# A mixture-of-experts decoder step on one core: gate/up weights in 16 KB runs, tokens gathered three expert blocks at a time

## The chip, the core and the metric

One core of a Trainium2 chip runs the whole step as one program. The metric is the device time of one execution in microseconds; the time of a kernel is the median of its runs. TensorE (PE) multiplies, VectorE (DVE), ScalarE (ACT) and GpSimd (POOL) work on tiles in SBUF and on TensorE's results in PSUM, SyncE (SP) only issues DMAs. Sixteen DMA engines move data between HBM and SBUF; each moves one contiguous piece, a packet in the profile, at a time.

## The reference, cut to what matters

One layer of a hybrid decoder over 336 rows (16 meta tokens and 256 prompt tokens, 8 sequences of 8 new tokens). A state-space branch and an attention branch are merged, projected and added to the residual; then a routed mixture of experts follows:

```python
hn = rmsnorm(h, norm2_g)                       # 336 x 1024
gsel = argmax(hn @ w_rg + b_rg)                # 1 of 4 groups
topl, topi = top_k(el_sel, 2)                  # 2 of its 8 experts
def block(tok, wr, e):                         # the rows that chose expert e
    xb = hn[tok]
    hb = silu(xb @ w_gate[e]) * (xb @ w_up[e])     # 1024 -> 512, twice
    return (hb @ w_down[e]) * wr[:, None]          # 512 -> 1024
```

There are 32 experts; everything is float32. An expert has 2.097 MB each of gate, up and down weights, 6.29 MB in all, and each expert in use is read once.

## The kernel before, in words

The program runs phases one after another: setup, state-space branch, attention, merge (`merge_phase`), routing (`route_phase`), experts (`moe_phase`) and the final norm. The 336 rows lie in three tiles of 128, 128 and 80 rows.

**Ahead of the experts.** `merge_phase` ends with the second norm. VectorE scales each row tile into `hn` (line 1318, named yT in the profile, whose memory it uses), waiting for GpSimd's root per tile (line 1279); TensorE transposes `hn` (1367), VectorE multiplies by `norm2_g` (1323) and TensorE computes the router's logits (1374). `norm2_g` comes to SBUF as 8 rows of 128 numbers in one of ten small loads on ScalarE's queue (line 188), for all of which TensorE waits at the very start; a transpose turns them into columns of `gcol`. `route_phase` chooses the experts and gives each pair of token and expert a slot: blocks of 64 slots, each block owned by one expert; GpSimd's iota instructions (1411 to 1418) are waited for there. In the input at hand 32 blocks are in use, one per expert.

**Weights.** SyncE issues all weight loads on one queue. `load_gate_up` (line 1534) issues two DMAs per expert, gate and up; partition p gets the rows p, 128 + p, 256 + p, ... of the 1024 x 512 matrix, that is eight pieces of 2 KB. `load_down` (1541) gives partition p rows of 1024 numbers, four pieces of 4 KB. There are three buffers for gate/up (the third lies in a reused tile named stretch) and two for down. The first three gate/up pairs and two downs are loaded ahead, by guess of the expert's number. Then `load(b, h)` (1601) issues block b's down once block b-2's results have been copied out (`y_ev`, line 1605), and block b+2's gate/up once block b-1's products have been read (`gu_free`, 1609); the first of these is block 3's (1614).

**A block.** All of it is unrolled per engine, with semaphores between the engines. TensorE: 8 x 2 products of gate/up into `ph` (1721); `gather_rows` for the next block, 3 x 2 products with a 0/1 matrix `block_rows` that picks the block's 64 rows of `hn` (1699, into px); two transposes of the hidden rows (1728); `gather_turn`, four transposes of the picked rows (1706); then 4 x 2 products with `w_down` (1736), after waiting for h_t, for the weights and for a free result bank. A float32 product shows as two records. Two products of 64 result rows each run side by side in the two halves of the array. ScalarE: tanh (1638), the copy of the picked rows px out of PSUM (1630), the copy of the result (1642) and its store, two DMAs of 128 KB. VectorE: `pick()` builds the next 0/1 matrix by comparing slots with an iota (1659, 1664); h_gate and h_rows (1681, 1684); the copy of h_t (1687); the scaling of the gathered, transposed rows by `norm2_g` (1669). Before the loop `pick`, `gather_rows(1)` and `gather_turn(1)` run once by themselves.

Of the kernel before, what the change touches and what calls it, by code (L numbers as in the profile page):

```python
# [14 lines left out]
F32 = mybir.dt.float32  # L15
# [6 lines left out]
P = 128  # L22
# [36 lines left out]
LEAST_BLK = 2 * T // BLK // 2 * 2  # L59


def bc(ap, shape):

    return ap.to_broadcast(list(shape))


def setup_phase(nc, A, S, sem):

    with ExitStack() as ctx:
# [3 lines left out]
        rows64 = tsb("param_rows", [64, P])  # L73
# [110 lines left out]
        def _(act):  # L184
# [3 lines left out]
            act.dma_start(rows64[56:64, :], A["norm2_g"].rearrange("a (t p) -> (a t) p", p=P)).then_inc(par_in, 16)  # L188
# [28 lines left out]
        def _(v):  # L217
# [9 lines left out]
            v.tensor_copy(S["gcol"][:, :], ps[6][:, 32:64])  # L227
# [70 lines left out]
        def _(pe):  # L298
            pe.wait_ge(consts, 1)
            pe.wait_ge(par_in, 160)  # L300
            pe.transpose(ps[6][:, 0:64], rows64[:, :], S["ident"][0:64, 0:64])
# [916 lines left out]
def merge_phase(nc, A, S, sem):  # L1218

    with ExitStack() as ctx:  # L1220
# [27 lines left out]
        def _(sp):  # L1248
# [12 lines left out]
            sp.dma_start(wr[:, :, 0:4], A["w_router_group"].rearrange("a (t p) c -> p (a t) c", p=P)).then_inc(wr_in, 16)  # L1261
            sp.dma_start(wr[:, :, 4:36], A["w_router_expert"].rearrange("a (t p) c -> p (a t) c", p=P)).then_inc(wr_in, 16)
# [33 lines left out]
        def _(v):  # L1296
# [19 lines left out]
            for t, r in enumerate(ROWS):  # L1316
                v.wait_ge(rs_ok, 3 + t + 1)
                v.tensor_scalar(S["hn"][0:r, t, :], S["xtok"][0:r, t, :], ss[0:r, t:t + 1], None,
                                ALU.mult).then_inc(hn_ok, 1)
            for t, r in enumerate(ROWS):  # L1320
                for h in range(2):
# [3 lines left out]
                                    bc(S["gcol"][:, 24 + 4 * h:28 + 4 * h].unsqueeze(2), [P, 4, r]),  # L1325
# [53 lines left out]
def route_phase(nc, A, S, sem):  # L1379


    with ExitStack() as ctx:
# [4 lines left out]
        it64i, itbi, itb = tsb("iota64_i", [P, BLK], I32), tsb("iota_blk_i", [1, NBLK], I32), tsb("iota_blk", [1, NBLK])  # L1387
# [158 lines left out]
def moe_phase(nc, A, S, sem):  # L1546
# [4 lines left out]
    with ExitStack() as ctx:  # L1551
        def tsb(name, shape, dt=F32):
# [4 lines left out]
        eq = tsb("slot_eq", [P, 3, 2, BLK])  # L1557
        sel = tsb("block_rows", [P, 3, BLK])
        xrow = tsb("x_rows", [P, 512])
        xg = tsb("x_gathered", [P, 4, 2, BLK])  # L1560
# [3 lines left out]
        px, pxt, ph, pht = (ctx.enter_context(nc.psum_tensor(n, [P, 512], F32)) for n in ("px", "pxt", "ph", "pht"))  # L1564
        py = [ctx.enter_context(nc.psum_tensor(f"py{h}", [P, 512], F32)) for h in range(2)]
        sel_ok, xr_ps, xr_ev, xt_ps, xt_ok, gu_ps, th_ok, hb_ok, ht_ps, ht_ok, y_ps, y_ev, gu_free = (
            sem(n) for n in ("sel_ok", "xrow_ps", "xrow_ev", "xt_ps", "xt_ok", "gu_ps", "hth_ok", "h_ok", "ht_t_ps",
# [5 lines left out]
        block = ctx.enter_context(nc.Block())  # L1573

        def blocks_of(eng):
            return eng.value_load(S["blk_e"][0:1, NBLK:NBLK + 1], min_val=1, max_val=NBLK)

# [46 lines left out]
        def _(act):  # L1624
            nblk = blocks_of(act)
            act.sem_inc(y_ev, 2)

            def rows_out(n):
                act.wait_ge(xr_ps, n)
                act.activation(xrow[:, :], px[:, :], ACT.Copy).then_inc(xr_ev, 1)  # L1630

            rows_out(1)
# [19 lines left out]
        def _(v):  # L1652
# [3 lines left out]
            def pick():  # L1656
# [3 lines left out]
                                bc(S["iota"][:, :].unsqueeze(1), [P, 6, BLK]),  # L1660
                                bc(rel[:, :, :].rearrange("p t j -> p (t j)").unsqueeze(2), [P, 6, BLK]),
# [3 lines left out]
                v.tensor_scalar(rel[:, :, :], rel[:, :, :], -float(BLK), None, ALU.add)  # L1665

            def gathered(n):
                v.wait_ge(xt_ps, n)
                v.tensor_tensor(xg[:, :, :, :], pxt[:, :].rearrange("p (c j s) -> p c j s", c=4, j=2),  # L1669
                                bc(S["gcol"][:, 24:32].rearrange("p (j c) -> p c j", j=2).unsqueeze(3),  # L1670
                                   [P, 4, 2, BLK]), ALU.mult).then_inc(xt_ok, 1)

            pick()
            gathered(1)
            with v.Fori(0, NBLK // 2) as i:
                for u in range(2):
                    b = 2 * i + u
                    with v.If(b < nblk):
                        pick()
# [5 lines left out]
                                               ALU.mult).then_inc(hb_ok, 1)  # L1685
                        v.wait_ge(ht_ps, b + 1)
                        v.tensor_copy(ht[:, :, :, :], pht[:, 0:256].rearrange("p (c j s) -> p c j s", c=2, j=2)
                                      ).then_inc(ht_ok, 1)
                        gathered(b + 2)

        @block.tensor
        def _(pe):
            nblk = blocks_of(pe)

            def gather_rows(n):
                pe.wait_ge(sel_ok, n)
                for t, r in enumerate(ROWS):
                    for j in range(2):
                        mm = pe.matmul(px[64 * j:64 * j + 64, :], sel[0:r, t, :], S["hn"][0:r, t, 512 * j:512 * j + 512],  # L1699
                                       start=(t == 0), stop=(t == 2))  # L1700
                mm.then_inc(xr_ps, 1)

            def gather_turn(n):
                pe.wait_ge(xr_ev, n)
                for c in range(4):
                    mm = pe.transpose(pxt[:, P * c:P * c + P], xrow[:, P * c:P * c + P], S["ident"][:, :])
                mm.then_inc(xt_ps, 1)
# [193 lines left out]
```

## Time and profile before

| what | before |
|---|---|
| median of 3 runs, us | 1550.07 (1548.98 to 1555.38) |
| span of the profiled execution, us | 1547.8 |
| PE busy / DVE / ACT / POOL | 87% / 32% / 17% / 13% |
| granted clock of TensorE, mean | 0.925 of full |
| SyncE's DMA queue | 232242 packets, 302.03 MB, 57.6% of 16 engines |
| issues of 2 MB expert weights | 32 gate, 32 up, 32 down |

The span reaches from the first to the last instruction of the profiled execution, and is the only time given for that execution; the median of the runs is 2.3 us longer. In the rows below, a line such as L1721 is a line of the kernel, `out<-in` names the tiles, "128*64 128x512" is a weight load of 64 columns with 512 moving columns, and a count stands behind x. SPq and ACTq are DMA issues on the queues of SyncE and ScalarE; their duration is the time the issue took, not the transfer. A granted clock of 1.00 is 2.4 GHz, 0.50 is 1.2 GHz.

### The profile page before, as it was taken

Reading aid. Unit: us, or ns where it says so; the run is one execution under the profiler, and the core shown is the slowest. Engines: PE = TensorE matmul, PEld = TensorE weight load, DVE = VectorE, ACT = ScalarE, POOL = GpSimd, SP = SyncE. Lnnn points to the kernel's source line nnn. Section 1 sums busy time; section 2 is a strip of 40 time slices with the busy share of each in tenths; the row PEclk is TensorE's granted clock in tenths of the full one; section 3 lists DMA queues with packets and bytes.
Section 4 is the critical chain, followed back from the end, with each engine's and each line's share of the span. In section 5 each row is a group of like instructions: output and inputs, shape, how many; then the busy total and the mean of one; then the engine's idle time right before and its main releaser. Section 6 shows DMA issues by size and latency. Waiting matters only on the chain. (4 is left out here: it accounts for less than half of the span.)

```text
span 1547.8 us, 19560 instructions
## 1 busy us (share of the span) xinstructions
PE 1339.0 (87%) x6097; PEld 738.9 (48%) x6097; DVE 492.3 (32%) x1106; ACT 263.9 (17%) x677; POOL 205.9 (13%) x401
## 2 busy tenths in 40 slices
PE   5799999999995997786999998499998899998990
PEld 3676667666672555554666654233332233332330
DVE  2245555556545673332000002421212112111113
ACT  1132223322330442221000000011100000010011
POOL 3032443334432120000000000000000000000003
PEclk9799999999996998998999999599999999999995
DMA  6033234424222238454865700789999999999974
GB/s 191 19 109 112 85 94 126 139 78 118 81 58 70 50 99 299 136 157 101 221 136 126 219 21 0 272 335 396 395 398 395 395 398 395 395 398 395 395 291 125
DMA packets 241057, 318.30 MB, mean 206 GB/s; under 512 B 21010, under 2 KB 148434, under 8 KB 241026
## 3 DMA queue, kind: packets, MB, share of 16 engines
q1 hardware_dynamic: 232242, 302.03, 57.6%
q10 hardware_dynamic: 6736, 8.94, 1.7%
q0 software_dynamic: 2048, 6.95, 1.7%
q8 instruction: 16, 0.26, 0.1%
q14 instruction: 15, 0.12, 0.0%
HBM read 289.20 MB, written 28.68 MB: 205 GB/s over the span
## 5 line engine op out<-in xcount | busy, mean ns | idle before, releaser
L667 PE MATMUL psg<-stretch 128*128 128x336 f32 x512 | 159.8, 477 | 11.3 <-DVE h_sample_out L645 9.6
L1736 PE MATMUL py<-w_down,h_t 128*64 128x512 f32 x512 | 135.6, 679 | 30.4 <-DMA w_down<-in_w_exp_down 30.4
L1721 PE MATMUL ph<-w_gate_up,x_gathered 128*64 128x512 f32 x704 | 157.2, 600 | 0.9 <-DVE x_gathered L1669 0.9
L667 PEld LDWEIGHTS psg<-stretch 128*128 128x128 f32 x512 | 103.7, 204 | 69.2 <-DVE h_sample_out L645 15.4
L1681 DVE SCALAR_TENSOR_TENSOR h_gate<-h_tanh,ph 128x256 f32<-128x256 f32 x32 | 13.5, 421 | 339.1 <-ACT h_tanh L1638 339.1
L1699 PE MATMUL px<-yT,block_rows 128*64 128x512 f32 (+1 forms) x396 | 93.3, 607 | 10.7 <-DVE block_rows L1664 10.7
L1721 PEld LDWEIGHTS ph<-w_gate_up,x_gathered 128*64 128x64 f32 x704 | 50.8, 139 | 104.1 <-issue 104.1
L582 DVE SCALAR_TENSOR_TENSOR x_conv<-x_padded,conv_wh,x_conv 128x360 f32<-128x360 f32 x96 | 57.0, 594 | 100.9 <-ACT x_conv L531 90.0
L1736 PEld LDWEIGHTS py<-w_down,h_t 128*64 128x64 f32 x512 | 38.3, 154 | 105.5 <-issue 69.9
L676 PE MATMUL psg<-stretch 128*128 128x256 f32 (+1 forms) x384 | 84.5, 380 | 0.0
L1343 PE MATMUL psm<-stretch,w_merge 128*128 128x336 f32 x256 | 76.2, 457 | 6.9 <-DMA w_merge<-in_w_in 6.9
L1773 POOL DMA_INDIRECT y_expert<-expert_rows,slot_i x6 | 5.7, 958 | 549.2 <-PEq L1743 547.7
L676 PEld LDWEIGHTS psg<-stretch 128*128 128x128 f32 (+1 forms) x384 | 67.3, 177 | 14.5
L1348 PE MATMUL psm<-yT,w_merge 128*128 128x336 f32 x256 | 73.6, 446 | 0.0
L1721 PE MATMUL ph<-stretch,x_gathered 128*64 128x512 f32 x320 | 70.4, 592 | 0.0
L1343 PEld LDWEIGHTS psm<-stretch,w_merge 128*128 128x128 f32 x256 | 49.9, 196 | 31.6 <-issue 8.9
L1304 DVE SCALAR_TENSOR_TENSOR mix_part<-gate_tanh,psm 128x336 f32<-128x336 f32 x16 | 7.3, 501 | 178.5 <-PE psm L1351 178.5
L1699 PEld LDWEIGHTS px<-yT,block_rows 128*64 128x64 f32 (+1 forms) x396 | 28.8, 140 | 68.2 <-issue 57.4
L1348 PEld LDWEIGHTS psm<-yT,w_merge 128*128 128x128 f32 x256 | 48.6, 190 | 23.7
L1091 PE MATMUL psa<-stretch,w_q 128*128 128x336 f32 x128 | 42.0, 486 | 15.0 <-DVE k_and_c L1000 12.6
L1642 ACT ACTIVATE y_block<-py 128x512 f32<-128x512 f32 x32 | 19.1, 597 | 192.2 <-PE py L1736 192.2
L1638 ACT ACTIVATE h_tanh<-ph 128x256 f32<-128x256 f32 x32 | 12.3, 384 | 203.4 <-PE ph L1721 203.4
(414 smaller groups left out, 1777.8 us busy)
## 6 DMA issues: line engine op xcount, KB each, us to landing
w_down<-in_w_exp_down SPq DMA_DIRECT2D x32, 2048.0 KB, 19.1
w_gate_up<-in_w_exp_gate SPq DMA_DIRECT2D x22, 2048.0 KB, 19.1
w_gate_up<-in_w_exp_up SPq DMA_DIRECT2D x22, 2048.0 KB, 22.9
stretch<-in_w_exp_gate SPq DMA_DIRECT2D x10, 2048.0 KB, 19.2
stretch<-in_w_exp_up SPq DMA_DIRECT2D x10, 2048.0 KB, 23.2
stretch<-in_w_in SPq DMA_DIRECT2D x16, 1024.0 KB, 5.3
stretch<-in_w_in SPq DMA_DIRECT2D x16, 512.0 KB, 7.5
h<-in_state_ssm SPq DMA_DIRECT2D x16, 512.0 KB, 4.9
```

What stands on the lines that cost most here:

```text
L582: i = v.scalar_tensor_tensor(xc[:, m, :], xp[:, m, w:w + 360], S["conv_wh"][:, w, bass.ds(o, 1)], xc[:, m, :], ALU.mult, ALU.add)
L667: mm = pe.matmul(ps[m][:, 0:T], wg[:, k, P * m:P * m + P], S["xnT"][:, k, :], start=(k == 0), stop=(k == KT - 1))
L676: mm = pe.matmul(ps[4 + t // 2][0:r, 256 * (t % 2):256 * (t % 2) + 256], S["xnT"][:, k, COL[t]:COL[t] + r], wg[:, k, 512:768], start=(k == ...
L1091: mm = pe.matmul(ps[0][:, 0:T], wq[:, k, :, :], S["xnT"][:, k, :], start=(k == 0), stop=(k == KT - 1))
L1343: mm = pe.matmul(ps[4 * h + j][:, 0:T], wm[h][:, 8 * j + k, :], S["xnT"][:, k, :], start=(k == 0), stop=(k == KT - 1))
L1348: pe.matmul(ps[4 * h + 2][:, 0:T], wm[h][:, 16 + k, :], S["yT"][:, k, :], start=(k == 0), stop=(k == 15))
L1638: act.activation(th[:, :], ph[:, 0:256], ACT.Tanh, scale=0.5).then_inc(th_ok, 1)
L1642: act.activation(yr[h][:, :], py[h][:, :], ACT.Copy).then_inc(y_ev, 1)
L1681: v.scalar_tensor_tensor(hg[:, :], th[:, :], 1.0, ph[:, 0:256], ALU.add, ALU.mult).then_inc(gu_free, 1)
L1699: mm = pe.matmul(px[64 * j:64 * j + 64, :], sel[0:r, t, :], S["hn"][0:r, t, 512 * j:512 * j + 512], start=(t == 0), stop=(t == 2))
L1721: mm = pe.matmul(ph[64 * j:64 * j + 64, :], xg[:, k % 4, k // 4, :], w_gu[w][:, :, k, 256 * j:256 * j + 256], start=(k == 0), stop=(k == K ...
L1736: mm = pe.matmul(py[h][64 * j:64 * j + 64, :], ht[:, k % 2, k // 2, :], w_dn[h][:, k, 512 * j:512 * j + 512], start=(k == 0), stop=(k == 3))
```

## The change

The rows of gate and up are dealt out differently: partition p now gets rows 8p to 8p+7, which lie behind one another in memory, so a load has one run of 16 KB per partition. The column order of `hn` follows (column k of partition p is 8p + k), by a strided read when `hn` is scaled, and so do the router's weights and `norm2_g`, which is now loaded directly as columns (`gcol2`). `load_down` is as before.

The gather is made for chunks of three blocks (192 slots) at once and without the turn: `hn` is the stationary operand, the 0/1 matrix of 192 columns the moving one, and the result arrives transposed, eight slices k of 128 partitions x 192 columns, three products each. The slices are dealt into six groups, two per block: one between gate/up and the transposes of the hidden rows, one between these and `w_down`. Two PSUM banks px0 and px1 alternate; VectorE scales each group into one of two buffers `x_gathered`. ScalarE's copy px to x_rows and TensorE's four transposes go. `pick` runs once per three blocks with three times the columns. Before the loop the whole first chunk is gathered.

```diff
+CHUNK = 3
+COLS = CHUNK * BLK
+GROUPS = ((0, 2), (2, 1), (3, 2), (5, 1), (6, 1), (7, 1))
...
-            act.dma_start(rows64[56:64, :], A["norm2_g"].rearrange("a (t p) -> (a t) p", p=P)).then_inc(par_in, 16)
+            act.dma_start(S["gcol2"][:, :], A["norm2_g"].rearrange("a (p t) -> (a p) t", p=P)).then_inc(par_in, 16)
...
-            sp.dma_start(wr[:, :, 4:36], A["w_router_expert"].rearrange("a (t p) c -> p (a t) c", p=P)).then_inc(wr_in, 16)
+            sp.dma_start(wr[:, :, 4:36], A["w_router_expert"].rearrange("a (p t) c -> p (a t) c", p=P)).then_inc(wr_in, 16)
...
-                v.tensor_scalar(S["hn"][0:r, t, :], S["xtok"][0:r, t, :], ss[0:r, t:t + 1], None,
+                v.tensor_scalar(S["hn"][0:r, t, :].rearrange("r (k p) -> r k p", k=KT),
+                                S["xtok"][0:r, t, :].rearrange("r (p k) -> r k p", k=KT), ss[0:r, t:t + 1], None,
                                 ALU.mult).then_inc(hn_ok, 1)
...
-            pool.iota(it64i[:, :], pattern=[[1, BLK]], base=0, channel_multiplier=0)
+            pool.iota(it64i[:, :], pattern=[[1, COLS]], base=0, channel_multiplier=0)
...
-        eng.dma_start(S["w_gate_up"][h][:, j, :, :], A[w].rearrange("a e (t p) f -> p (a e) t f", p=P)[
-            :, bass.ds(e, 1)].rearrange("p o t f -> p (o t) f")).then_inc(done, 16)
+        eng.dma_start(S["w_gate_up"][h][:, j, :, :].rearrange("p t f -> p (t f)"), A[w].rearrange("a e (p t) f -> p (a e) (t f)", p=P)[
+            :, bass.ds(e, 1)].rearrange("p o f -> p (o f)")).then_inc(done, 16)
...
+        def bank(g):
+            k0, n = GROUPS[g]
+            return px[g % 2][:, 0:n * COLS].rearrange("p (k s) -> p k s", k=n)
...
-                        rows_out(b + 2)
...
+            def gathered(chunk, parity, g):
+                k0, n = GROUPS[g]
+                v.wait_ge(xg_ps, n_groups * chunk + g + 1)
+                v.tensor_tensor(xg[parity][:, k0:k0 + n, :], bank(g),
+                                bc(S["gcol2"][:, k0:k0 + n].unsqueeze(2), [P, n, COLS]), ALU.mult).then_inc(xg_ok, 1)
 
             pick()
-            gathered(1)
-            with v.Fori(0, NBLK // 2) as i:
-                for u in range(2):
-                    b = 2 * i + u
+            for g in range(n_groups):
+                gathered(0, 0, g)
+            pick()
+            with v.Fori(0, NBLK // 6) as i:
+                for u in range(6):
+                    b, chunk, a, parity = 6 * i + u, 2 * i + u // 3 + 1, 2 * (u % 3), (u // 3 + 1) % 2
                     with v.If(b < nblk):
-                        pick()
                         v.wait_ge(th_ok, b + 1)
...
+                        gathered(chunk, parity, a)
                         v.wait_ge(ht_ps, b + 1)
...
-                        gathered(b + 2)
+                        gathered(chunk, parity, a + 1)
+                        if u % 3 == 2:
+                            pick()
...
+            def gather(chunk, g):
+                k0, n = GROUPS[g]
+                if g == 0:
+                    pe.wait_ge(sel_ok, chunk + 1)
+                pe.wait_ge(xg_ok, n_groups * chunk + g - 1)
+                for k in range(n):
+                    for t, r in enumerate(ROWS):
+                        mm = pe.matmul(bank(g)[:, k, :], S["hn"][0:r, t, P * (k0 + k):P * (k0 + k) + P],
+                                       sel[0:r, t, :], start=(t == 0), stop=(t == 2))
+                mm.then_inc(xg_ps, 1)
...
-                                mm = pe.matmul(ph[64 * j:64 * j + 64, :], xg[:, k % 4, k // 4, :],
+                                mm = pe.matmul(ph[64 * j:64 * j + 64, :],
+                                               xg[u // 3][:, k, BLK * (u % 3):BLK * (u % 3) + BLK],
                                                w_gu[w][:, :, k, 256 * j:256 * j + 256],
                                                start=(k == 0), stop=(k == KT - 1))
                         mm.then_inc(gu_ps, 1)
-                        gather_rows(b + 2)
+                        gather(chunk, a)
                         pe.wait_ge(hb_ok, b + 1)
...
-                        gather_turn(b + 2)
+                        gather(chunk, a + 1)
                         pe.wait_ge(ht_ok, b + 1)
```

## Rows read from the trace of the kernel before

**Rows 1.** The page, the span in 40 equal slices: GB/s moved.

```profile
GB/s 191 19 109 112 85 94 126 139 78 118 81 58 70 50 99 299 136 157 101 221 136 126 219 21 0 272 335 396 395 398 395 395 398 395 395 398 395 395 291 125
```

**Rows 2.** Busy time by stretch (us busy, instructions), granted clock, DMA share, GB/s.

```profile
960.00:1000.00 40.00, 19.72 (x84) 14.62 (x86) 15.18 (x59) 1.01 (x3) 1.40 (x7) 0.50 0.71 263
1000.00:1010.00 10.00, 10.00 (x38) 3.08 (x36) 0.99 (x4) 0.38 (x1) 0.00 (x0) 0.79 0.00 0
...
1060.00:1460.00 400.00, 364.89 (x1628) 122.67 (x1624) 71.85 (x170) 38.80 (x75) 0.00 (x0) 0.95 1.04 396
...
985.00:988.00 3.00, 0.00 (x0) 0.00 (x0) 2.85 (x4) 0.00 (x0) 0.00 (x0) 0.50 1.02 405
...
989.50:993.50 4.00, 2.14 (x6) 0.77 (x8) 1.26 (x4) 0.00 (x0) 0.00 (x0) 0.50 1.04 386
```

**Rows 3.** Waits of 1000 to 1547 us: us in total, times, longest one.

```profile
PE py L1736 <- DMA w_down<-in_w_exp_down: 30.4, 22, 2.1
```

**Rows 4.** Timeline of a block: start us, us, engine, line, tiles, [idle before].

```profile
1016.24 7.04 PE L1721 MATMUL ph<-w_gate_up,x_gathered 128*64 128x512 f32 x32
...
1023.10 2.75 PE L1699 MATMUL px<-yT,block_rows 128*64 128x512 f32 x12
...
1024.25 0.42 DVE L1684 SCALAR_TENSOR_TENSOR h_rows<-h_gate,ph 128x256 f32<-128x256 f32 x1
...
1025.78 0.44 PE L1728 MATMUL pht<-ident,h_rows 128*128 128x128 f32 x2
...
1027.14 3.65 PE L1736 MATMUL py<-w_down,h_t 128*64 128x512 f32 x16
...
1030.62 0.60 PE L1721 MATMUL ph<-stretch,x_gathered 128*64 128x512 f32 x2
```

**Rows 5.** Timeline of SyncE's queue: five gate/up issues and one w_down.

```profile
970.79 3.98 SPq L1542 DMA_DIRECT2D w_down<-in_w_exp_down  x1
974.81 2.10 SPq L1537 DMA_DIRECT2D stretch<-in_w_exp_gate  x1
...
1009.96 0.39 SPq L1537 DMA_DIRECT2D w_gate_up<-in_w_exp_gate  x1
...
1100.99 1.62 SPq L1537 DMA_DIRECT2D w_gate_up<-in_w_exp_gate  x1
...
1464.45 1.63 SPq L1537 DMA_DIRECT2D w_gate_up<-in_w_exp_gate  x1
1466.19 7.93 SPq L1537 DMA_DIRECT2D w_gate_up<-in_w_exp_up  x1
```

**Rows 6.** DMA issues, 965 to 1000 us: KB each, us to landing.

```profile
w_down<-in_w_exp_down SPq DMA_DIRECT2D x1, 2048.0 KB, 18.2
stretch<-in_w_exp_gate SPq DMA_DIRECT2D x1, 2048.0 KB, 19.6
```

**Rows 7.** TensorE groups by line and shape: busy us, mean ns, idle.

```profile
L676 PE MATMUL psg<-stretch 128*128 128x256 f32 x256 | 56.8, 380 | 0.0
...
L1351 PE MATMUL psm<-stretch,w_merge 128*128 128x336 f32 x128 | 37.5, 446 | 0.0
```

**Rows 8.** Timeline of 990 to 1000 us: first selection, first row products, first block.

```profile
990.31 0.56 DVE L1659 TENSOR_TENSOR slot_eq<-iota,slot_rel 128x384 f32<-128x384 f32 x1
990.94 0.36 DVE L1664 TENSOR_TENSOR block_rows<-slot_eq 128x192 f32<-128x192 f32 x1
...
991.36 5.39 PE L1699 MATMUL px<-yT,block_rows 128*64 128x512 f32 x12 [10.66 <-DVE block_rows L1664]
...
999.42 9.47 PE L1721 MATMUL ph<-w_gate_up,x_gathered 128*64 128x512 f32 x32 [0.86 <-DVE x_gathered L1669]
```

**Rows 9.** Timeline: scaling of the third row tile; a small first load.

```profile
955.90 0.75 DVE L1318 TENSOR_SCALAR yT<-xtok,ss 80x1024 f32<-80x1024 f32 x1 [0.86 <-POOL ss L1279]
...
5.39 0.80 ACTq L193 DMA_DIRECT2D brow<-in_b_forget  x1
```

**Rows 10.** The page, DMA queues: packets, MB, share of 16 engines over the span.

```profile
q8 instruction: 16, 0.26, 0.1%
```

More of the change, by code:

```diff
@@ L71, in tsb @@
             return ctx.enter_context(nc.sbuf_tensor(name, shape, dt))
-        rows64 = tsb("param_rows", [64, P])
+        rows64 = tsb("param_rows", [56, P])
         convw_rows = tsb("convw_rows", [P, P])
@@ L1556, in moe_phase @@
         rel = tsb("slot_rel", [P, 3, 2])
[L1557 to L1560, printed above, removed]
+        eq = tsb("slot_eq", [P, 3, 2, COLS])
+        sel = tsb("chunk_rows", [P, 3, COLS])
+        xg = [tsb(f"x_gathered{c}", [P, KT, COLS]) for c in range(2)]
         th, hg, hrow = tsb("h_tanh", [P, 256]), tsb("h_gate", [P, 256]), tsb("h_rows", [P, 256])
@@ L1563, in moe_phase @@
         yr = [tsb(f"y_block{h}", [P, 512]) for h in range(2)]
-        px, pxt, ph, pht = (ctx.enter_context(nc.psum_tensor(n, [P, 512], F32)) for n in ("px", "pxt", "ph", "pht"))
+        ph, pht = (ctx.enter_context(nc.psum_tensor(n, [P, 512], F32)) for n in ("ph", "pht"))
+        px = [ctx.enter_context(nc.psum_tensor(f"px{h}", [P, 512], F32)) for h in range(2)]
         py = [ctx.enter_context(nc.psum_tensor(f"py{h}", [P, 512], F32)) for h in range(2)]
-        sel_ok, xr_ps, xr_ev, xt_ps, xt_ok, gu_ps, th_ok, hb_ok, ht_ps, ht_ok, y_ps, y_ev, gu_free = (
-            sem(n) for n in ("sel_ok", "xrow_ps", "xrow_ev", "xt_ps", "xt_ok", "gu_ps", "hth_ok", "h_ok", "ht_t_ps",
+        sel_ok, xg_ps, xg_ok, gu_ps, th_ok, hb_ok, ht_ps, ht_ok, y_ps, y_ev, gu_free = (
+            sem(n) for n in ("sel_ok", "xg_ps", "xg_ok", "gu_ps", "hth_ok", "h_ok", "ht_t_ps",
                              "ht_ok", "yb_ps", "yb_ev", "gate_up_free"))
@@ L1659, in pick @@
                 v.tensor_tensor(eq[:, :, :, :].rearrange("p t j c -> p (t j) c"),
-                                bc(S["iota"][:, :].unsqueeze(1), [P, 6, BLK]),
-                                bc(rel[:, :, :].rearrange("p t j -> p (t j)").unsqueeze(2), [P, 6, BLK]),
+                                bc(S["iota"][:, :].unsqueeze(1), [P, 6, COLS]),
+                                bc(rel[:, :, :].rearrange("p t j -> p (t j)").unsqueeze(2), [P, 6, COLS]),
                                 ALU.is_equal)
@@ L1693, in _ @@
             nblk = blocks_of(pe)
[L1695 to L1707, printed above, removed]
-            gather_rows(1)
-            gather_turn(1)
+            def gather(chunk, g):
[8 more added lines that the diff above has]
+                mm.then_inc(xg_ps, 1)
+            pe.wait_ge(sel_ok, 1)
+            for g, (k0, n) in enumerate(GROUPS):
+                if g > 1:
+                    pe.wait_ge(xg_ok, g - 1)
+                for k in range(n):
+                    for t, r in enumerate(ROWS):
+                        mm = pe.matmul(bank(g)[:, k, :], S["hn"][0:r, t, P * (k0 + k):P * (k0 + k) + P],
+                                       sel[0:r, t, :], start=(t == 0), stop=(t == 2))
+                mm.then_inc(xg_ps, 1)
             with pe.Fori(0, NBLK // 6) as i:
@@ L1713, in _ @@
                     b, h, w = 6 * i + u, u % 2, u % 3
+                    chunk, a = 2 * i + u // 3 + 1, 2 * (u % 3)
                     with pe.If(b < nblk):
-                        pe.wait_ge(xt_ok, b + 1)
+                        if u % 3 == 0:
+                            pe.wait_ge(xg_ok, n_groups * chunk)
                         pe.wait_ge(w_ok, b + 1)
@@ L1815, in sb @@
             S[name] = stack.enter_context(nc.sbuf_tensor(name, shape, dt))
-        for name, shape in (("ident", [P, P]), ("ones", [P, P]), ("mhalf", [P, 4]), ("gcol", [P, 32]),
+        for name, shape in (("ident", [P, P]), ("ones", [P, P]), ("mhalf", [P, 4]), ("gcol", [P, 24]), ("gcol2", [P, KT]),
                             ("xtok", [P, 3, D]), ("yT", [P, 16, T]), ("topw", [P, 3, 2]), ("slot", [P, 3, 2]),
-                            ("iota", [P, BLK])):
+                            ("iota", [P, COLS])):
             sb(name, shape)
```

22 lines of the change are left out of this document (7 added, 15 removed).

## The prediction, made before the changed kernel was run

> **What bounds the kernel now.** I read the page's forty slices first, for which resource is flat. From the 28th slice the bytes per second stand at 395 to 398 for eleven slices in a row [rows 1]; nothing ahead of them is so even. Second, busy time by stretch: from 1060 to 1460 us the DMA engines are busy throughout (a share of 1.04, since packets overlap) and move 396 GB/s, while TensorE is busy for 365 of 400 us at a granted clock of 0.95; from 1000 to 1010 nothing is moved at all [rows 2]. Third, the waits: TensorE waits 22 times, 30.4 us, for `w_down` [rows 3]. Fourth, one block before the DMA falls behind: gate/up to gate/up takes 1030.62 - 1016.24 = 14.38 us at full clock [rows 4]. Fifth, SyncE's issues: from the 7th gate load (1100.99) to the 29th (1464.45) lie 22 blocks in 363.46 us, 16.52 us each, and one up load holds the queue for 7.93 us, which I read as a queue that is full [rows 5]. So a block needs 14.38 us of TensorE and gets its weights every 16.52 us. The expert stage, a third of the span, is bound by the rate at which weights arrive. It runs at that pace from the first load after the prefetch, at 1009.96 [rows 5], which is when block 0's gate/up products have been read. From there 29 gate and 29 up loads follow one another without a hole; the tail behind them the change leaves as it is.
>
> **Gate/up runs of 16 KB.** Each 2.097 MB load keeps its bytes and goes from 1024 pieces of 2 KB to 128 of 16 KB: from 64 pieces to 8 on each of 16 engines. What a piece costs must come from pieces of different length. The prefetch before the stage gives it, with no other traffic and TensorE all but idle. By issue plus landing time, `w_down` (4 KB runs, 32 pieces per engine) lands at 970.79 + 18.2 = 989.0, the third slot's gate (2 KB) at 974.81 + 19.6 = 994.4, so the stretch 985 to 988 is `w_down` alone and 989.5 to 993.5 the gate alone: 405 against 386 GB/s [rows 2, 5, 6]. A load therefore takes 5.178 us at 4 KB and 5.433 us at 2 KB; 0.255 us for 32 pieces is 8.0 ns a piece. At 8 pieces a load would take 5.178 - 24 x 0.0080 = 4.99 us (420 GB/s, an extrapolation by four in length). Saving: 0.446 us a load, x 58 = **-25.9 us**. Bounds: if nothing is gained beyond 4 KB, 0.255 x 58 = -14.8; if each of the two rates is off by 1 GB/s so that they lie further apart, the same working gives some -28.5. The check: two gate/up loads, one `w_down` and 0.26 MB of result rows at the 2 KB rate make 16.72 us against the 16.52 observed. After the change the block's transfers need 16.52 - 0.89 = 15.63 us.
>
> The row puts the step from 2 to 4 KB at 4.9%. The Trainium skill ("DMA: Bandwidth & Descriptors", Why small descriptors are slow) says that a packet costs about 3 extra cycles beside one per 32 bytes. That is 67 cycles for 64 at 2 KB and 515 for 512 at 16 KB; by it a load falls from 5.433 to an estimated 5.22 us, 58 of them save 12.4 us, and the step to 4 KB should have been 2.3%: the trace shows twice that.
>
> **Gathering three blocks at once.** It lies on TensorE, VectorE and ScalarE, under the transfers. Removed per block: six row products (from 1023.10 to the h transposes at 1025.78, 2.68 us), four transposes behind them (of the 1.36 us to 1027.14, 0.6), ScalarE's copy. Added per three blocks: 24 products of 192 columns. The nearest rows are 256 columns, 56.8 us for 128 products (two records each), 0.444 us, and 336 columns, 37.5 for 64, 0.586 us [rows 7]; the line through them gives 0.33 us at 192. The first two blocks of three get nine, 14.38 - 2.68 - 0.6 + 2.97 = 14.07 us; the third gets six, of which only three (0.99 us) cover the chain tanh, h_gate, h_rows that ends at 1024.67, 1.57 us after gate/up [rows 4], so TensorE stands 0.6 to 0.7 us: 13.74. Mean 13.96 us, under the 15.63 of the transfers: **0**. Low clock must be added: a clock of 0.95 over 400 us is 40 us at half speed, 20 us lost over 24 blocks, 0.8 each; 14.8 is still below 15.63. If that cover went (low clock twice as often), TensorE would set the pace near 15.6, where the forecast is anyway. VectorE's new wait for the gathered columns stands ahead of its copy of h_t, for which TensorE waits: in a nine-product block the columns are there some 2.0 us after gate/up, scaling 384 costs about 0.56 like the 384 of [rows 8], the copy 0.42 like h_rows; that ends near 3.0, when TensorE (2.0 + 0.44 + 0.99) is still in its second group. In the third block the group is half as long. VectorE is busy 72 of 400 us [rows 2] and has room. On SyncE the order of loads and waits stays; shorter lists of pieces fill its queue less, and it then waits for `gu_free` or `y_ev` instead, with only the next load behind it.
>
> **The first gather.** This one nothing hides: no load is in flight from 1000 to 1010, and every microsecond delays 1009.96. The two selection instructions have three times the elements: 384 cost 0.56 and 192 cost 0.36 us, so 1152 and 576 cost 1.36 and 0.76, +1.2 us [rows 8]. Then 24 products where 12 records in 5.39 us, a copy, transposes and a scaling took until 999.42 [rows 8]. The clock was 0.50 up to 1000, and 0.79 from 1000 to 1010 [rows 2], so it rose near 1004.2, 4.8 us after gate/up began. If it rises 4.8 us into the new unbroken stream: 7.3 products at 0.66 and 16.7 at 0.33 take 10.3 us; block 0 begins at 991.36 + 1.2 + 10.3 + 0.6 (last scaling) = 1003.5 and ends, at full speed, 7.04 later, 1010.5, against 999.42 + 9.47 = 1008.9 now: +1.6. If it stays low: 15.8 us for the gather, 9.47 for block 0, +9.5. I take **+3**, near the first because the pauses between 996.75 and 999.42, in which the old stream waited for the copy and the scaling, are gone.
>
> **Serial edits.** The scaling of the rows reads every eighth column. 1024 contiguous columns take 0.75 us and the third instruction waits 0.86 us for GpSimd [rows 9]; at one element a cycle, which VectorE's 1.04 ns per element [rows 8] shows, 1024 would take 1.1 to 1.3: the first two eat the slack, the third adds 0.5. **+0.8**, between 0 and, if the stride halves the rate again, +3.5. The norm2_g load becomes 128 pieces of 32 B among ten small loads that TensorE waits for; a broadcast load of as many pieces takes 0.80 us to issue [rows 9], and less was spent before: +0.3, ends 0 and +0.8. GpSimd's wider iota and cast stand before the routing: all its work in those 40 us is 1.40 us [rows 2], so at most a few tenths, +0.2. The router's weights are loaded long before their use: 0. **Tail:** TensorE's last block is some 0.4 us shorter: -0.4.
>
> **Sum.** -25.9 + 3 + 1.3 - 0.4 = -22.0 us. The profiled execution's span is 1547.8 us, so its new span is 1525.8. The median of the runs is 1550.07, 2.3 us above that span; I keep this and forecast **1528 us**.
>
> **Rivals.** *Runs stop paying at 4 KB* (the engines cut a longer run, or something else caps near 405): -14.8 + 3.9 = -10.9, 1539. For it: no load of this kernel shows more than 405 in an undisturbed stretch. Chance 0.14. *The overhead is half of what I read*, because 3 us of `w_down` are a small sample: 12.9 saved, 1541; 0.07. By the 3-cycle rule of the Trainium skill ("DMA: Bandwidth & Descriptors", Why small descriptors are slow) this one would be the forecast. *The bytes set the rate, not the pieces*: then no load gets shorter and the start and serial edits remain, +3.9, 1554. Against it stand 405 and 386 in one trace; 0.07. The Trainium skill ("DMA: Bandwidth & Descriptors", Where 436 GB/s comes from) says that HBM, at about 358 GB/s a core, binds such loads; by it 1554 would be right, but the 396 GB/s held here for 400 us lie above its limit. *Slower: a 16 KB piece is served worse.* The place is each gate/up load. The only 16 KB packets in the trace are the instruction queue's: 16, 0.26 MB, 0.1% of 16 engines' span [rows 10]; 0.1% is 24.8 us, 1.55 us a packet, and with the rounding at least 0.77 us, 339 GB/s over 16 engines. A load would take 6.19 us, 58 x 0.76 = +44, 1598 at the least. Against it: those packets shared their engines with other queues and go elsewhere. It decides from 5.46 us a load (384 GB/s): above that, 58 x 0.03 + 3.9 pass 0.5%. Chance 0.08. *More than forecast*: a piece costs more than 8 ns, or the clock rises at once, 1518; 0.05. That leaves 0.59 for the forecast.
>
> **Numbers.** A measurement of this kernel can tell 0.5%, 7.75 us, from no change: below 1542.3 is faster, above 1557.8 slower. Faster: 0.59 + 0.14 x 0.9 + 0.07 x 0.6 + 0.05 = 0.80. Slower 0.08. Same 0.12: the no-gain case and the edges of the two small ones. Range 1517 to 1542: the forecast with its bounds (-28.5 + 1.6 up to -14.8 + 3.9), the 4 KB case, about half of the 1541 case and most of the 1518 case hold some 0.8.
>
> **What would show it.** Right: steady slices near 16.52/15.63 x 396 = 419 GB/s, 57,344 fewer packets, gate loads 15.6 us apart, TensorE still waiting for `w_down`, about 1.6 us a block less the low clock, block 0's gate/up starting at 1003 to 1006. The 4 KB rival would show 408; no gain, 396; the slow one, less, with longer waits. Wrong: waits at `w_down` gone and blocks 15 us or more apart (TensorE bound), the first load past 1016, or a gap in the loads.

## The result, and the profile after

The changed kernel takes 1526.01 us, the median of four runs (1524.47 to 1528.54), beside 1550.44 (1548.98 to 1555.38) for the kernel before: a ratio of 0.984, 95% interval 0.982 to 0.986. The forecast was 1528, the range 1517 to 1542. The span of the profiled execution went from 1547.8 to 1522.8 us, 25.0 less.

First the forty slices of the changed kernel's page, GB/s moved, beside [rows 1].

```profile
GB/s 194 19 111 101 99 83 141 114 86 97 127 59 58 49 47 306 150 155 66 257 134 138 116 187 0 151 234 422 424 420 427 419 426 421 426 421 423 425 301 127
```

The plateau is still there and still flat, so the same resource bounds the stage; it stands at 419 to 427 where it stood at 395 to 398. The windows say the same beside [rows 2] (per engine us busy and instructions, then granted clock, DMA share, GB/s):

```profile
1000.00:1010.00 10.00, 9.38 (x51) 7.71 (x52) 4.75 (x9) 0.00 (x0) 0.00 (x0) 0.95 0.09 35
1010.00:1060.00 50.00, 49.73 (x246) 24.69 (x244) 10.36 (x23) 3.33 (x7) 0.00 (x0) 1.00 0.87 354
1060.00:1460.00 400.00, 364.21 (x1728) 165.40 (x1726) 72.34 (x157) 25.52 (x52) 0.00 (x0) 0.98 1.02 423
```

423 GB/s in the steady stretch against 396; TensorE busy for 364 us as before, but for more blocks. SyncE's queue moved the same 302.03 MB in 174,898 packets instead of 232,242: 57,344 fewer, 896 for each of the 64 loads. Next the waits from 1000 to 1547 us (us in total, times, longest), beside [rows 3]:

```profile
DVE x_gathered L1672 <- PE px L1708: 29.9, 54, 0.8
...
PE py L1749 <- DMA w_down<-in_w_exp_down: 33.3, 19, 2.1
...
PE pht L1741 <- DVE h_rows L1687: 2.8, 10, 0.3
```

TensorE still waits for `w_down`, no less than before: both sides of the race became faster. The one large new wait is VectorE's for the gathered columns, and nobody is late for it: h_t and the hidden rows are waited for 2.8 us in all. One block, beside [rows 4], in the timeline of TensorE, of the changed kernel:

```profile
1021.70 7.07 PE L1733 MATMUL ph<-w_gate_up,x_gathered 128*64 128x512 f32 x32
1028.70 2.22 PE L1708 MATMUL px<-chunk_rows,yT 128*128 128x192 f32 x12
1030.76 0.38 PE L1741 MATMUL pht<-ident,h_rows 128*128 128x128 f32 x2
1030.98 1.14 PE L1708 MATMUL px<-chunk_rows,yT 128*128 128x192 f32 x6
1032.09 3.65 PE L1749 MATMUL py<-w_down,h_t 128*64 128x512 f32 x16
1035.55 7.07 PE L1733 MATMUL ph<-stretch,x_gathered 128*64 128x512 f32 x32
1042.54 1.24 PE L1708 MATMUL px<-chunk_rows,yT 128*128 128x192 f32 x6
1044.06 0.44 PE L1741 MATMUL pht<-ident,h_rows 128*128 128x128 f32 x2 [0.27 <-DVE h_rows L1687]
```

Gate/up to gate/up takes 13.85 us where it took 14.38. The third block of a chunk (from 1035.55) has the short first group, and there TensorE stands 0.27 us for the hidden rows. SyncE's queue, beside [rows 5]: the 1st, 7th and 29th gate load, one up load, and the load that ends the stage (`final_g`, the final norm's vector, issued when SyncE is through with the expert stage).

```profile
1015.98 0.35 SPq L1541 DMA_DIRECT2D w_gate_up<-in_w_exp_gate  x1
...
1097.98 0.33 SPq L1541 DMA_DIRECT2D w_gate_up<-in_w_exp_gate  x1
...
1435.69 0.33 SPq L1541 DMA_DIRECT2D w_gate_up<-in_w_exp_gate  x1
1436.12 0.38 SPq L1541 DMA_DIRECT2D w_gate_up<-in_w_exp_up  x1
...
1493.65 0.36 SPq L1771 DMA_DIRECT2D final_g<-in_final_norm_g  x1
```

The first loads are 13.67 us apart (six intervals in 82.00 us), TensorE's pace, while the prefetched stock lasts; the 7th to the 29th lie 15.35 us apart, the 13th to the 29th 15.50 (16.52 before). No up load holds the queue any longer: 0.38 us to issue, not 7.93. Reading note: the median from issue to landing rose from 19 to 23 or 24 us for a gate load, though the stage moves more bytes per second. I read that as an earlier start of the count: an issue no longer waits for room in the queue, so it is made while earlier loads are still under way.

The accounting of the 25.0 us uses two marks, the first gate load (1009.96 before [rows 5], 1015.98 now) and the issue of `final_g`. Of the kernel before it needs three more lines, the start of the scaling, the copy of the slots and `final_g`:

```profile
953.64 1.41 DVE L1318 TENSOR_SCALAR yT<-xtok,ss 128x1024 f32<-128x1024 f32 x2
...
990.06 0.17 DVE L1654 COPY slot_rel<-slot 128x6 f32<-128x6 f32 x1 [1.22 <-PEq L1382]
...
1518.41 0.36 SPq L1758 DMA_DIRECT2D final_g<-in_final_norm_g  x1
```

From the first gate load to the issue of `final_g`, which I call the stage, it was 1518.41 - 1009.96 = 508.45 us and is 477.67: **-30.8**. The first load itself went from 1009.96 to 1015.98: **+6.0**. Behind `final_g`: -0.2. Of the +6.0, 3.45 are there before any edited instruction of this part runs: the scaling of `hn` starts at 957.09 instead of 953.64, and in the other profiles below it starts anywhere from 952.42 to 961.58, with the old order of rows and the new; what makes it scatter stays open. The rest is seen in the timeline of the start, beside [rows 8, 9]:

```profile
957.09 2.21 DVE L1321 TENSOR_SCALAR yT<-xtok,ss 128x1024 f32<-128x1024 f32 x2
960.09 1.14 DVE L1321 TENSOR_SCALAR yT<-xtok,ss 80x1024 f32<-80x1024 f32 x1 [0.79 <-POOL ss L1282]
...
994.87 0.17 DVE L1656 COPY slot_rel<-slot 128x6 f32<-128x6 f32 x1 [1.22 <-PEq L1386]
995.12 1.36 DVE L1661 TENSOR_TENSOR slot_eq<-iota,slot_rel 128x1152 f32<-128x1152 f32 x1
996.55 0.76 DVE L1666 TENSOR_TENSOR chunk_rows<-slot_eq 128x576 f32<-128x576 f32 x1
...
997.37 9.85 PE L1718 MATMUL px<-chunk_rows,yT 128*128 128x192 f32 x48 [11.86 <-DVE chunk_rows L1666]
```

The three scalings end 4.14 us after their start, 3.01 before (+1.13). From there to the copy of the slots: 33.64, 33.41 before (+0.23, the wider iota). From that copy to the end of block 0's gate/up (1007.83 + 7.09): 20.05, 18.83 before (+1.22). Together +2.6.

### The profile page after: what moved, and what is told of

It is laid out like the page before. It is cut to its first block and busy times, and to the rows that moved or that the text cites. A ratio compares the mean times of both kernels' runs of the same rounds, so it can differ in the third digit from the quotient of the medians.

```text
span 1522.8 us, 19514 instructions
## 1 busy us (share of the span) xinstructions
PE 1315.7 (86%) x6133; PEld 791.9 (52%) x6133; DVE 490.5 (32%) x1080; ACT 244.2 (16%) x644; POOL 207.1 (14%) x401
## 3 DMA queue, kind: packets, MB, share of 16 engines
q1 hardware_dynamic: 174898, 302.03, 55.6%
## 5 line engine op out<-in xcount | busy, mean ns | idle before, releaser
L1749 PE MATMUL py<-w_down,h_t 128*64 128x512 f32 x512 | 125.0, 632 | 33.4 <-DMA w_down<-in_w_exp_down 33.3
L1708 PE MATMUL px<-chunk_rows,yT 128*128 128x192 f32 x516 | 97.9, 332 | 0.0
L1708 PEld LDWEIGHTS px<-chunk_rows,yT 128*128 128x128 f32 x516 | 82.4, 190 | 26.0 <-issue 26.0
```

The costliest lines, as they stand in the source:

```text
L1708: mm = pe.matmul(bank(g)[:, k, :], S["hn"][0:r, t, P * (k0 + k):P * (k0 + k) + P], sel[0:r, t, :], start=(t == 0), stop=(t == 2))
L1749: mm = pe.matmul(py[h][64 * j:64 * j + 64, :], ht[:, k % 2, k // 2, :], w_dn[h][:, k, 512 * j:512 * j + 512], start=(k == 0), stop=(k == 3))
```

## Experiments

In each, "stage" and "first load" are the two marks above; the first load is counted from the start of the `hn` scaling, since what lies ahead of that scatters (56.32 us before, 58.89 after).

**The runs alone.** The kernel before with the new order of rows and none of the gather:

```diff
+        eng.dma_start(S["w_gate_up"][h][:, j, :, :].rearrange("p t f -> p (t f)"), A[w].rearrange("a e (p t) f -> p (a e) (t f)", p=P)[
...
+                v.tensor_scalar(S["hn"][0:r, t, :].rearrange("r (k p) -> r k p", k=KT),
```

> The kernel before with 16 KB gate/up runs (and the row order that goes with them), gathering block by block as before. Theory: the runs alone carry the gain, since the gather lies under the transfers; the changed kernel's blocks come every 15.50 us against 16.52, and TensorE's 14.38 us plus some 0.8 us of low clock still fit. The first gather of the change (block 0's gate/up read 1.4 us later than the row scaling alone explains) is missing, so about 1525 us, 1522 to 1528. Rival, the shorter gather carries the gain: about 1550. Rival, both are needed, because TensorE at 14.38 us becomes the bound: 1532 or more, with waits for w_down gone.

Measured 1519.99 us, ratio 0.980 (0.977 to 0.983), below the changed kernel's median and below what was expected. Its steady window:

```profile
1060.00:1460.00 400.00, 375.28 (x1752) 128.41 (x1748) 77.69 (x184) 41.43 (x79) 0.00 (x0) 1.00 1.01 423
```

And its queue of SyncE: the 1st and 29th gate load, and the end of the stage.

```profile
1008.42 0.35 SPq L1538 DMA_DIRECT2D w_gate_up<-in_w_exp_gate  x1
...
1427.86 0.33 SPq L1538 DMA_DIRECT2D w_gate_up<-in_w_exp_gate  x1
...
1486.34 0.36 SPq L1759 DMA_DIRECT2D final_g<-in_final_norm_g  x1
```

The same 423 GB/s, and a stage of 477.92 us, equal to the changed kernel's 477.67. From the 1st to the 29th gate load it took 419.44 us, with the gather 419.71: the old gather's blocks keep TensorE's pace of 14.38 us for thirteen intervals, the new one's 13.7 for eight, and both take the same time in all, since the transfers decide. **The runs carry the whole gain.** The first load comes 54.49 us after the scaling starts, 4.4 earlier than in the changed kernel.

**The gather alone.** The changed kernel with the loads and the order of rows of before:

```diff
-        eng.dma_start(S["w_gate_up"][h][:, j, :, :].rearrange("p t f -> p (t f)"), A[w].rearrange("a e (p t) f -> p (a e) (t f)", p=P)[
-            :, bass.ds(e, 1)].rearrange("p o f -> p (o f)")).then_inc(done, 16)
+        eng.dma_start(S["w_gate_up"][h][:, j, :, :], A[w].rearrange("a e (t p) f -> p (a e) t f", p=P)[
+            :, bass.ds(e, 1)].rearrange("p o t f -> p (o t) f")).then_inc(done, 16)
```

> The changed kernel with gate/up in 2 KB runs as before (and the plain row order). Theory: no gain, and the start costs 1.4 us: 1551 to 1553, steady blocks 16.5 us apart, longer waits for w_down than before (TensorE's block is shorter, the transfers are not). Rival, the shorter gather carries the gain: 1526 to 1535.

Measured 1553.55 us, ratio 1.002 (0.9995 to 1.004). Its steady window:

```profile
1060.00:1460.00 400.00, 354.06 (x1629) 156.00 (x1629) 67.33 (x147) 24.15 (x49) 0.00 (x0) 0.95 1.04 396
```

And TensorE's wait for the weights from 1000 to 1547 us:

```profile
PE py L1748 <- DMA w_down<-in_w_exp_down: 49.4, 24, 3.1
```

396 GB/s as before; the 0.7 us a block that TensorE saves come back as longer waits for `w_down`, 49.4 us for 30.4. The stage is 507.49 us, 1.0 less; its two marks on SyncE's queue:

```profile
1018.25 0.39 SPq L1540 DMA_DIRECT2D w_gate_up<-in_w_exp_gate  x1
...
1525.74 0.36 SPq L1770 DMA_DIRECT2D final_g<-in_final_norm_g  x1
```

**Runs of 4 KB and of 8 KB.** The changed kernel with the rows dealt out in u groups of t = 2 (then 4) neighbouring rows per partition; `norm2_g`, the router's weights and the columns of `hn` follow:

```diff
+        eng.dma_start(S["w_gate_up"][h][:, j, :, :].rearrange("p (u t) f -> p u (t f)", t=2), A[w].rearrange("a e (u p t) f -> p (a e) u (t f)", p=P, t=2)[
+            :, bass.ds(e, 1)].rearrange("p o u f -> p (o u) f")).then_inc(done, 16)
```

> The changed kernel with gate/up dealt out in 4 KB runs, 4 per partition: 32 pieces per engine and load in place of 8. Theory, every piece costs the same 9.1 ns (1.02 us a block for 112 pieces, from the changed kernel's blocks): 58 x 24 x 9.1 ns = +12.7 us, about 1539. Rival, runs stop paying at 4 KB: 1526, as the changed kernel. Rival, half the cost per piece: 1532.

> The same with 8 KB runs, 16 pieces per engine and load. Theory: 58 x 8 x 9.1 ns = +4.2 us, about 1530. Rival, runs stop paying at 4 KB: 1526. Rival, half the cost per piece: 1528.

Measured 1535.88 us (ratio 0.991, 0.987 to 0.994) and 1529.12 (0.986, 0.983 to 0.990). The steady window at 4 KB, and at 8 KB:

```profile
1060.00:1460.00 400.00, 360.83 (x1684) 161.78 (x1684) 69.61 (x153) 24.53 (x50) 0.00 (x0) 0.96 1.03 411
```

```profile
1060.00:1460.00 400.00, 367.67 (x1717) 164.03 (x1718) 72.56 (x158) 25.49 (x52) 0.00 (x0) 0.96 1.02 419
```

The stage shows it without the scatter of the phases ahead. Its marks at 4 KB, and at 8 KB:

```profile
1018.83 0.39 SPq L1543 DMA_DIRECT2D w_gate_up<-in_w_exp_gate  x1
...
1509.75 0.36 SPq L1773 DMA_DIRECT2D final_g<-in_final_norm_g  x1
```

```profile
1016.83 0.39 SPq L1543 DMA_DIRECT2D w_gate_up<-in_w_exp_gate  x1
...
1498.27 0.36 SPq L1773 DMA_DIRECT2D final_g<-in_final_norm_g  x1
```

| run | pieces of a load per engine | stage, us | saved, us | per piece (saved / pieces / 58) |
|---|---|---|---|---|
| 2 KB (gather alone) | 64 | 507.49 | | |
| 4 KB | 32 | 490.92 | 16.57 | 8.9 ns |
| 8 KB | 16 | 481.44 | 9.48 | 10.2 ns |
| 16 KB (the change) | 8 | 477.67 | 3.77 | 8.1 ns |

A piece costs much the same at every length: 29.82 / 56 / 58 = 9.2 ns over all. What halves from step to step is the number of pieces. The rival that nothing is gained beyond 4 KB falls with the last two lines. The theory's times, from 9.1 ns a piece, were 1 to 3 us too long; at 4 KB, 1.1 us of that is the scaling of `hn`, which reads every second column there and takes 3.0 us as before, not 4.1. The price is what a piece adds to the stage, not a pause between two pieces: an engine's packets overlap, as the DMA shares of 1.02 and 1.03 above show. Whether it arises in reading short runs of memory or in handling each packet no run separates, since run length and number of packets always changed together.

**`w_down` in 8 KB runs.** Two neighbouring rows of `w_down` per partition and run; VectorE writes the hidden rows in the order that fits.

```diff
+    eng.dma_start(S["w_down"][h][:, :, :].rearrange("p (j c) d -> p j (c d)", j=2), A["w_exp_down"].rearrange("a e (j p c) d -> p (a e) j (c d)", p=P, j=2)[
...
+                        v.scalar_tensor_tensor(hrow[:, :].rearrange("p (c i) -> p i c", c=2),
+                                               hg[:, :].rearrange("p (i c) -> p i c", c=2), 0.5,
+                                               ph[:, 256:512].rearrange("p (i c) -> p i c", c=2), ALU.mult,
```

On the runs alone:

> The kernel before with the 16 KB runs (the old gather kept) and, besides, w_down in two runs of 8 KB per partition in place of four of 4 KB. Theory: a piece costs about 9.2 ns of DMA time whichever tensor it belongs to; 30 down loads with 16 pieces fewer on each engine save 30 x 16 x 9.2 ns = 4.4 us, so 1515.5 us beside 1520 for the 16 KB runs alone, a ratio to the kernel before of about 0.977, and gate loads 0.15 us closer together (15.3 us). Rival: the transfers are near a ceiling that piece length no longer moves, or TensorE's 14.4 us per block plus its low clock already set the pace: 1520, no change. Slower rival: writing the hidden rows to every second column lengthens the chain that TensorE waits for, by 0.1 to 0.4 us a block if nothing covers it: 1520 plus up to 12.

On the changed kernel:

> The changed kernel with w_down in two runs of 8 KB per partition. Theory (a piece costs 9.2 ns, transfers set the pace): 1526 - 4.4 = 1521.6 us, loads 15.35 us apart where 15.50 was seen, TensorE's waits for w_down smaller but still there. Rival (ceiling reached): 1526. Slower rival (the strided write of the hidden rows comes onto the path): up to 1538.

And the changed kernel itself beside them:

> The changed kernel itself, on the same chip as the others of this set, to set its time against that of the runs alone. Theory: the gather brings nothing under the transfers and costs about 4 us ahead of the first load, so this is about 1526 us beside 1520 for the 16 KB runs with the old gather (ratio to the kernel before 0.984 against 0.980). Rival: the 6 us between the two were scatter of the phases ahead, and both come out alike.

Measured, beside 1550.68 for the kernel before: 1515.47 us (ratio 0.978, 0.9765 to 0.980), 1518.22 (0.980, 0.9775 to 0.982) and 1525.18 (0.984, 0.983 to 0.986). With the old gather and with the new one the stage falls by 4.1 and 4.2 us (477.92 to 473.85, 477.63 to 473.46): 30 loads x 16 pieces at 8.5 and 8.7 ns, so the price is the piece's, not the tensor's. The repeat of the changed kernel gives its ratio again, 0.984. The runs alone were not repeated in this set; with `w_down` in 8 KB, both gathers side by side, the new one is 2.8 us behind in the medians, with intervals that overlap.

**The first gather twice.** TensorE makes the 24 products once more ahead of the real ones:

```diff
             pe.wait_ge(sel_ok, 1)
+            for g, (k0, n) in enumerate(GROUPS):
+                for k in range(n):
+                    for t, r in enumerate(ROWS):
+                        pe.matmul(bank(g)[:, k, :], S["hn"][0:r, t, P * (k0 + k):P * (k0 + k) + P],
+                                  sel[0:r, t, :], start=(t == 0), stop=(t == 2))
```

> The changed kernel; TensorE makes the 24 products of the first gather once more ahead of the real ones, whose results overwrite them. Theory: nothing covers the work between the selection matrix and the first load, so what these 24 products take (about 8 us at full clock, up to 16 at half) is added in full, less what block 0 gains if its clock rises earlier: 1526 + 8 = 1534 us or more, the first load later by as much, steady rate unchanged at 423 GB/s. Rival: the stage makes up for a late start, because early blocks are paced by TensorE and the prefetched buffers are full: 1526 to 1529.

Measured 1533.73 us, 8.55 above the changed kernel on the same chip. The timeline:

```profile
993.99 9.91 PE L1716 MATMUL px<-chunk_rows,yT 128*128 128x192 f32 x48 [11.85 <-DVE chunk_rows L1666]
1003.74 7.99 PE L1723 MATMUL px<-chunk_rows,yT 128*128 128x192 f32 x48
1012.35 7.09 PE L1738 MATMUL ph<-w_gate_up,x_gathered 128*64 128x512 f32 x32 [0.62 <-DVE x_gathered L1672]
```

The first load comes 66.77 us after the scaling starts, 7.88 later than in the changed kernel, and the stage stays 477.48. Nothing covers the first gather: the 7.99 us of the second pass come back as 7.88 at the first load and, within the scatter, as 8.55 of the whole. The second pass runs at full clock; the first took 9.91, since the clock rises while it runs (granted 0.50 from 993 to 996 us, 0.71 to 999, 1.00 from there to the end of the pass).

**More work for TensorE.** Three, then eight, further 192-column products per block, into a bank that nobody reads:

```diff
                         gather(chunk, a + 1)
+                        for z in range(3):
+                            pe.matmul(pz[:, 0:COLS], S["hn"][:, 0, 0:P], S["hn"][:, 0, 0:COLS], start=True, stop=True)
                         pe.wait_ge(ht_ok, b + 1)
```

> The changed kernel with three more 192-column products per block on TensorE (332 ns each, 1.0 us), written to a bank that nobody reads. Theory: the transfers set the pace at 15.5 us and TensorE needs 13.7 us plus at most 0.8 for low clock, so 14.7 to 15.5 us still fits; only the first two or three blocks, which run on prefetched weights, pay their 1.0 us: 1526 to 1530, loads 15.5 us apart, waits for w_down smaller. Rival: TensorE already sets the pace of the changed kernel: 31 blocks x 1.0 = 1557.

> The changed kernel with eight more such products per block (2.66 us). Theory: 13.7 + 2.66 = 16.4 us per block is now above the 15.5 us of the transfers and TensorE sets the pace; 31 blocks at 16.4 make 508 us where the stage took 478: about 1556 us, waits for w_down gone, DMA at about 400 GB/s. If the low clock stays besides, up to 0.8 x 24 more: 1575. Rival: TensorE's real need is smaller than its timeline shows and the time stays near 1530; rival: TensorE set the pace before: 1526 + 82 = 1608.

Three cost nothing that can be measured, 1523.14 us (ratio 0.985, 0.982 to 0.987). The steady window keeps its 423 GB/s with TensorE busy for 386 us instead of 364:

```profile
1060.00:1460.00 400.00, 385.84 (x1908) 186.76 (x1906) 72.32 (x157) 26.08 (x53) 0.00 (x0) 1.00 1.02 423
```

They use up TensorE's waits (1000 to 1547 us):

```profile
PE py L1752 <- DMA w_down<-in_w_exp_down: 12.2, 15, 1.1
```

The waits fall from 33.3 to 12.2 us, the stage is 479.17 (+1.5). Eight turn the kernel over to TensorE, 1566.90 us (1.011, 1.008 to 1.0135). The steady window, and then two gate/up starts in the timeline of TensorE:

```profile
1060.00:1460.00 400.00, 397.79 (x2022) 214.94 (x2019) 68.23 (x149) 24.13 (x50) 0.00 (x0) 1.00 1.00 404
```

```profile
1302.99 7.04 PE L1734 MATMUL ph<-w_gate_up,x_gathered 128*64 128x512 f32 x32
...
1319.40 7.04 PE L1734 MATMUL ph<-w_gate_up,x_gathered 128*64 128x512 f32 x32
```

TensorE has no idle time left, `w_down` no longer stands among its waits, a block takes 16.41 us (15.9 for the third of a chunk). The direction was as expected, the size 11 us short: I had put 31 blocks into the stage, and from the first load to `final_g` it holds nearly 32 (517.74 us at a mean of 16.25). So the changed kernel has between 1.0 and 2.7 us of TensorE time a block to spare; 15.50 less 13.67, 1.8 us, lies between.

**`w_down` in 16 KB runs too**, on the runs alone. A half of the hidden columns is then made of pairs of weight columns:

```diff
+    eng.dma_start(S["w_down"][h][:, :, :].rearrange("p c d -> p (c d)"), A["w_exp_down"].rearrange("a e (p c) d -> p (a e) (c d)", p=P)[
...
-                                               w_gu[w][:, :, k, 256 * j:256 * j + 256],
+                                               w_gu[w][:, :, k, :].rearrange("p o (q m) -> p o q m", m=4)[:, :, :, 2 * j:2 * j + 2],
```

> The kernel before with 16 KB runs for gate, up and w_down alike (old gather). For w_down a partition then holds four neighbouring rows, so the gate/up products of a half take two of every four weight columns. Theory: 30 x 8 more pieces saved on each engine at 9.2 ns, 2.2 us below the version with w_down in 8 KB runs (1515.5): 1513.3, if TensorE reads its moving columns in pairs as fast as in one run. Rival: the broken runs slow the products: the 7.1 us of a block's gate/up grow, and past about 0.9 us more a block TensorE sets the pace, 31 us for each further us.

Measured 1514.50 us, ratio 0.977 (0.9756 to 0.979), which cannot be told from 0.978. The timeline says why:

```profile
1302.31 7.37 PE L1724 MATMUL ph<-stretch,x_gathered 128*64 128x512 f32 x32
...
1317.02 7.37 PE L1724 MATMUL ph<-w_gate_up,x_gathered 128*64 128x512 f32 x32
```

Gate/up takes 7.37 instead of 7.04 us, the block 14.71, and TensorE keeps that pace for 22 intervals in a row, to the load at 1340.16, and waits for `w_down` only 3.8 us in all: the two sides are almost even. The stage is 472.74, 1.1 less instead of 2.2.

## Why the prediction was right, and where it was off

| step | predicted, us | measured, us |
|---|---|---|
| runs, 58 loads | -25.9 | -30.5 (stage, runs alone) |
| gather under the transfers, tail | 0, -0.4 | -1.0 together (stage, gather alone) |
| first gather | +3, ends +1.6 and +9.5 | +1.2 in the pair of profiles, +4.2 beside the runs alone |
| `hn` scaling, iota | +0.8, +0.2 | +1.1, +0.2 |
| `norm2_g` load | +0.3 | 0.0 (its issue takes 0.37 us for 0.30, but TensorE's first long products start at 21.31 us, 21.29 before) |

**The bound** was read rightly. Flat bytes per second, TensorE waiting for `w_down`, and a block of TensorE shorter than the interval of the loads: the three extra products confirm it from one side, the eight from the other.

**The runs** had the right mechanism and too small a price, and this is the largest miss: 8.0 ns a piece, from two stretches of 3 and 4 us in the prefetch, against 9.2 ns in the stage. The shorter stretch was hardly `w_down` alone, as I took it: in its last us, 987 to 988, 387 GB/s were moved, already the gate's rate. One us earlier, 984 to 987, the same trace gives 411 GB/s and by the same working 10.3 ns, so the two rows could not tell 8 from 10. A load saves 30.5 / 58 = 0.53 us, not 0.446. The saving lies beyond even the bound of -28.5 that I drew from 1 GB/s of error in each rate, where moving the stretch by one us changes the rate by 6. Steady rate 423 against 419 forecast, loads 15.5 us apart against 15.6. The extrapolation by four in length held: 10.2 and 8.1 ns a piece for its two halves. By an estimate from the 3-cycle rule of the Trainium skill ("DMA: Bandwidth & Descriptors", Why small descriptors are slow) 12.4 us would have been saved; the trace does not agree, it shows two and a half times that. The HBM limit of some 358 GB/s a core in the same page of the Trainium skill (Where 436 GB/s comes from) did not bind here: this one core held 423 GB/s for 400 us. As a rival it was read without its condition, since that page gives the figure (Bandwidth, Measured) as each core's share when both cores of an HBM domain stream.

**The gather** was rightly put at nothing under the transfers. TensorE's block was forecast at 13.96 us and is 13.67 over the first six intervals. Of the parts, the 192-column product came at 0.33 us as forecast (24 in 7.99 us at full clock, first gather twice); the standing in the third block was overstated, 0.28 us for 0.6 to 0.7. VectorE's new wait did no harm, as worked out. The low clock was less than allowed for, 0.98 where 0.95 was kept.

**The first gather** came, at 1.2 us in the pair, just under the lower of its ends (+1.6 to +9.5), and within them at 4.2 beside the runs alone. The selection took 1.36 and 0.76 us, as forecast to the hundredth. The products took 9.85 us (10.3 forecast) and block 0 ran at full clock, 7.09 us. How much that is worth depends on the old kernel's own start, which I had from one execution: there block 0 ran in 9.47 us, in the runs alone in 7.09 and with `w_down` in 8 KB in 8.78, with the same instructions ahead of it. From the copy of the slots to the end of block 0 the old gather took 18.8, 15.9 and 17.3 us, the new one 19.9 to 20.6 in four profiles (the change, its repeat, with `w_down` in 8 KB, and the gather alone). So the cost is 1.2 to 4.2 us; +3 was a fair middle.

**The sum** of the measured parts for the profiled pair is -30.8 + 2.6 - 0.2 = -28.4 where -22.0 was forecast. That the median came within 2 us of the forecast owes something to chance: the phases ahead were 3.45 us later in the changed kernel's profile, and in later runs the kernel before alone ranges from 1544.6 to 1556.5. The same 3.45 us put two of the signs at the edge: block 0's gate/up starts at 1007.83 where 1003 to 1006 was named, and the first load at 1015.98 where past 1016 would have meant wrong.

**The rivals.** That runs stop paying at 4 KB is refuted by the 8 and 16 KB steps, the smaller overhead and the case without gain by the stage's 30 us, the slower 16 KB piece by 423 GB/s. One threshold of that last rival was worked out wrongly: 5.46 us a load give 58 x 0.03 + 3.9 = 5.6 us, which does not pass 0.5%, 7.75 us; it takes 5.50. The case "more than forecast", 1518, was the nearest to the truth of the runs by themselves.

**Better than both.** The 16 KB runs with the old gather and `w_down` in 8 KB runs take 1515.47 us, 0.978 of the kernel before; its interval ends below the changed kernel's.

## What to carry to other kernels

Where a stage's bytes per second are flat, price the pieces of a transfer apart from its bytes, over the whole stage and from two lengths; the price then carries to other lengths and tensors, until the next engine's time per block is reached. Time saved on an engine that waits only empties a stock of prefetched data sooner, and a larger unit of work there costs its first, uncovered instance in full. Compare stages by marks inside the trace when the phases ahead of them scatter by more than the effect.

## What the runs showed of the hardware that was not expected

- A load of few pieces does not hold SyncE's queue: 0.38 us for an up load of 128 pieces, also behind others. With 1024 pieces the first up load of the stage took 0.53 us to issue (at 1010.45, with only its gate load under way), the later ones, behind others, 1.4 to 10.4 (7.93 in [rows 5]). With the order of loads kept, no gain from it can be told apart here.
- The scaling that reads every eighth float32 takes 1.14 us for 1024 columns instead of 0.75, half again as long. The cost sets in between a step of two and one of four: every second column still takes 0.75 us (runs of 4 KB), every fourth 1.13 (runs of 8 KB).
- Moving columns in pairs, two of every four, slow a float32 product little: 7.37 us for 32 records against 7.04.
- The granted clock from 1060 to 1460 us was 1.00 in the kernels whose TensorE waited for `w_down` least (17.2 us with the runs alone, 12.2 with three extra products) and 0.95 in the one that waited most (49.4, the gather alone). It isn't a strict order: 0.95 before with 30.4 us of waiting, 0.98 after with 33.3. Which waits lower it was not tried.
